# VectorE takes a token block's forget gates one step later in the projection of a hybrid decoder trunk

## The reference, cut to what matters

```
h = rms_norm(x, norm_pre) * (1 + scale) + shift
u = h @ w_in
q, k, v, f_logit, z_rwkv, p_pool, g = jnp.split(u, IN_IDX, axis=-1)
...
log_f = jax.nn.log_sigmoid(f_logit + f_bias)     # 8 forget gates a token, one for each attention head
...
zf = z_rwkv
zf = zf + (token_shift(zf) - zf) * mu            # each token's column is mixed with that of the token before
```

## Time and profile before

| | |
|---|---|
| median of 3 runs | 3588.36 us |
| lowest, highest | 3586.56 us, 3593.07 us |
| the profiled execution's own time | 3581.05 us |
| its span, first to last instruction | 3579.3 us |
| TensorE busy | 3312.7 us, 93% of the span |
| VectorE busy | 2415.0 us, 67% |
| ScalarE busy | 1970.1 us, 55% |
| GpSimd busy | 1785.0 us, 50% |
| mean granted TensorE clock | 0.96 of full speed |

### The profile page before, as it was taken

One profiled execution on the slowest core, in us unless ns is written; L12 is line 12 of the kernel. 1 busy time (PEld: TensorE's weight loads), 2 busy tenths in 40 slices (PEclk: granted clock), 3 DMA queues, 4 the chain that ended last, 5 costly groups with the idle time before them and its releaser, 6 DMA issues. The chain is left out here.

```text
span 3579.3 us, 90138 instructions
## 1 busy us (share of the span) xinstructions
PE 3312.7 (93%) x31944; PEld 2298.4 (64%) x31944; DVE 2415.0 (67%) x4337; ACT 1970.1 (55%) x3745; POOL 1785.0 (50%) x2083
## 2 busy tenths in 40 slices
PE   6788999999999994999998699999999999979998
PEld 6783488469549642888888366666666656644444
DVE  5787756326433335786873789899889988965554
ACT  2444544424432234676775477777777777753333
POOL 2376300510330233344553599889988889852222
PEclk9899999999999997898997899999999999989999
DMA  7387445435444533232210312021120220215555
GB/s 313 129 300 254 161 146 169 151 130 178 146 141 155 181 133 89 57 84 69 67 49 28 70 43 59 9 57 36 29 59 10 55 49 17 58 70 181 186 186 180
DMA packets 247770, 401.06 MB, mean 112 GB/s; under 512 B 85646, under 2 KB 199013, under 8 KB 232453
## 3 DMA queue, kind: packets, MB, share of 16 engines
q1 hardware_dynamic: 223979, 383.75, 33.5%
q10 hardware_dynamic: 22880, 11.54, 1.2%
q0 software_dynamic: 480, 0.14, 0.1%
HBM read 272.77 MB, written 122.59 MB: 110 GB/s over the span
## 5 line engine op out<-in xcount | busy, mean ns | idle before, releaser
L2530 ACT ACTIVATE p<-psc,xb,sc 128x512 f32<-128x512 f32 (+3 forms) x1152 | 848.5, 744 | 315.1 <-PE psc L2621 302.1
L2508 POOL TENSOR_TENSOR plo<-p 128x512 f16<-128x512 f32 (+2 forms) x864 | 906.8, 1078 | 66.9 <-ACT p L2530 65.8
L2677 DVE TENSOR_REDUCE mx<-pm 128x1 f32<-128x512 f32 (+3 forms) x1201 | 731.4, 636 | 99.4 <-PE pm L2552 85.8
L646 PE MATMUL bank<-h,ring 128*128 128x512 f16 x2688 | 597.8, 381 | 4.9 <-DVE u L990 4.9
L2600 PE MATMUL po<-v,p 128*128 128x129 f16 x4224 | 513.3, 220 | 20.9 <-POOL plo L2508 18.0
L651 PE MATMUL bank<-ring,h 128*128 128x128 f16 x8064 | 467.0, 222 | 26.7 <-ACT c L818 12.3
L646 PEld LDWEIGHTS bank<-h,ring 128*128 128x128 f16 x2688 | 263.9, 98 | 343.4 <-issue 42.5
L2602 PE MATMUL po<-v,plo 128*128 128x65 f16 x4224 | 483.4, 192 | 0.0
L651 PEld LDWEIGHTS bank<-ring,h 128*128 128x128 f16 x8064 | 463.6, 99 | 28.1 <-issue 12.6
L2600 PEld LDWEIGHTS po<-v,p 128*128 128x128 bf16 x4224 | 388.8, 97 | 121.3 <-POOL plo L2508 28.0
L2602 PEld LDWEIGHTS po<-v,plo 128*128 128x128 f16 x4224 | 379.2, 98 | 96.2
(11 more groups left out here) (417 smaller groups left out, 5583.3 us busy)
## 6 DMA issues: line engine op xcount, KB each, us to landing
ring<-scratch_ws SPq DMA_DIRECT2D x52, 1792.0 KB, 7.8
scratch_z<-stage SPq DMA_DIRECT2D x72, 256.0 KB, 3.2
scratch_ws<-h SPq DMA_DIRECT2D x10, 1792.0 KB, 6.7
y<-scratch_y SPq DMA_DIRECT2D x35, 512.0 KB
g<-scratch_g SPq DMA_DIRECT2D x35, 512.0 KB
xr<-in_x SPq DMA_DIRECT2D x34, 512.0 KB, 6.2
scratch_g<-stage SPq DMA_DIRECT2D x64, 256.0 KB, 6.0
scratch_qk<-stage SPq DMA_DIRECT2D x64, 256.0 KB, 2.6
```

The costliest lines, as they stand in the source:

```text
L646: t = nc.tensor.matmul(bank[b][:], m.ring[:, slot, l, bo, k, :], hh[:, side, r, ao, k, :], start=fresh and first, stop=last, skip_group_ch ...
L2508: nc.gpsimd.tensor_tensor(plo[:, k % NP, 0:w], p32[:, k % NP, 0:w], hi[:, 0:w], ALU.subtract)\
L2530: nc.scalar.activation(p32[:, k % NP, 0:w], psc[k % 2][:, 0:w], ACT.Exp, bias=xb[:, u, b, x // 4:x // 4 + 1], scale=m.sc[:, 0:1]).then_inc ...
L2677: nc.vector.tensor_reduce(mx[:, s, t, q:q + 1], pm[g][:, 0, 0:w], AX.X, ALU.max).then_inc(pm_d.sem, 1)
```

## The change

The call of `forget` for a token block moves from VectorE's step g, the block's step 0, to step g+1. There it stands behind the shifts of that step, which are those of the last two z tiles of the preceding block. Both lists of VectorE hold the same instructions.

```
@@ -1105,10 +1105,10 @@
                     if group_at(g - 1, 3) is not None:
                         x_scaled(*group_at(g - 1, 3))
-                    if at is not None:
-                        if at[1] == 0:
-                            forget(at[0])
-                        elif at[2] == 1:
+                    if sub(g - 1) is not None and sub(g - 1)[1] == 0:
+                        forget(sub(g - 1)[0])
+                    if at is not None and at[1]:
+                        if at[2] == 1:
                             first_sum(at[0], at[1])
                         elif at[2] == 2:
                             second_sum(at[0], at[1])
```

## The result

| | before | changed |
|---|---|---|
| median | 3588.19 us, 8 runs | 3568.61 us, 8 runs |
| lowest, highest | 3572.18, 3605.60 us | 3557.29, 3576.50 us |
| the profiled execution's own time, its span | 3581.05, 3579.3 us | 3563.71, 3562.0 us |
| mean granted clock in the profiled execution | 0.960 | 0.961 |

The ratio is 0.9946, with a 95% interval from 0.9921 to 0.9972: the change makes the kernel faster, by 19.6 us between the medians. 11.2 us were forecast.

What follows compares the result with a forecast made beforehand. TensorE, busy for 93% of the span, was taken to bound the kernel; 7.0 us of idle time plus 4.2 us of clock, 11.2 us, off the median 3588.36 gave 3577.2 us, range 3570 to 3586.

Steps and rivals of the forecast that it cites:

- Which wait bounds, and what replaces it: Boundaries of blocks 1 to 3: ScalarE's copy would wait for TensorE alone, idle time falling from 3.67 to 1.33 us.
- The term of 2.34 us a boundary: TensorE's idle time behind step 0 in blocks 1 to 3: 2.34 us saved at each, 7.0 us in all.
- The shifts, the gates, the stores: Projection boundaries: shifts run 12 us sooner, forget gates run during ScalarE's copies, stores go out early; gates and stores cost 0.
- The clock, 4.2 us: Behind step 0 of blocks 1 to 3: of 5.9 us lost to half clock, 4.2 us come back.
- one of the three falls: Clock at the boundaries of blocks 1 to 3: one fall to half clock still happens, at 1.7 us.
- the wrong row to fear: Block 0, where the clock fell behind 1.33 us of idle time: nearest row, saying none of the clock loss returns.
- The sum: Projection: 7.0 us of idle time plus 4.2 us of clock, 11.2 us saved in all.
- How the numbers follow, the scatter: Whole kernel: range 3570 to 3586 us, its lower end from 12.9 us of gain and some 4 us of scatter.
- The second term of the range: Whole kernel: a gain of at most 12.9 us, used for the range's lower end.
- The slower rival: Later stages, 1377 to 1900 us: more half-clock stretches, about 1.7 us per fall; 3596 us with eleven; chance 0.08.
- eleven more falls: Later stages: eleven additional clock falls at about 1.7 us each would bring the time to 3596 us.
- The chances: Whole kernel: 0.61 faster (a time under 3581.2 us), 0.31 the same, 0.08 slower.

Runs made afterwards that it cites:

- filled kernel: The kernel before with 11 matmuls added on TensorE behind step 0 in token blocks 1 to 3; medians 3570.85 us (ratio 0.9961) and 3584.58 us (0.9970).
- e3: The changed kernel, with SyncE holding the stores of the preceding block's last two z tiles until TensorE has ended step 0; one run, 3572.44 us.
- e6: The changed kernel ended behind the projection, with x copied to the output instead of the later stages; median 1411.72 us.
- e10: The changed kernel run again as a plain copy with a profile; median 3573.26 us, ratio 0.9932 to the kernel before.
- e12: The changed kernel run once more as a plain copy; median 3576.73 us, ratio 0.9949 to the kernel before.
- e13: The changed kernel run yet again as a plain copy; median 3580.46 us, ratio 0.9956 to the kernel before.
- e5: The kernel before ended behind the projection, with x copied to the output instead of the later stages; median 1424.03 us.
- e9: The kernel before run again as a plain copy with a profile; median 3586.63 us, ratio 0.9994 to the other runs of the same kernel.
- e1: The kernel before with the forget gates moved to the later step in token block 1 alone; one run, 3594.57 us.

## Why the prediction was right and where it was wrong

*Which wait bounds, and what replaces it*: right. All three boundaries now look as block 0 did, with TensorE as the releaser and 1.27 us of idle time (1.33 in block 0). The term of 2.34 us a boundary measured 2.40 by rows, 2.41 by block 3 of the filled kernel.

*The shifts, the gates, the stores*: right. The shifts of the last two tiles begin 10.6, 12.4 and 12.9 us before the end of step 0 (12 forecast), and the gates run beside the copies at no cost. The stores left SyncE at 474.51 in block 1, and ScalarE had to wait for their landing until 485.29, 1.81 us instead of 0.96; TensorE did not notice, and neither did it in e3. From issue to landing the early stores of 256 KB took 10.0 us behind 2.8 MB of loads; in the kernel before, issued at 484.13, they took 2.0. The rule of the Trainium skill that a ring is served in order ("DMA: Bandwidth & Descriptors", section "Queues, rings and completion order") would have it so, and the trace agrees.

*The clock, 4.2 us*: right in kind, off in both halves. I took one of the three falls to stay. None did, in any of five profiles of the changed projection (the first, e6, e10, e12, e13), so the boundaries gave back all that was lost there: 4.79 − 2.40 = 2.4 us in block 1, 4.04 − 2.40 = 1.6 in block 3, and in block 2, by its undisturbed length of 296.24, also 300.26 − 296.24 − 2.40 = 1.6; 5.6 to 5.7 in all, against 5.9 taken. Yet a fall came elsewhere in each of these profiles, behind the 2 us of idle time at about 630 or 925 us, once in four of them and twice in e13, and took 1.4 to 1.9. The kernel before kept its clock at both places in its first profile (the earlier trace rows and the line at 933 us above) and in e5; in e9 it lost it at 634 us. Counted over all profiles, that is 1 of 6 such places in the kernel before and 14 of 24 in the twelve profiles of kernels that have no fall at the boundaries. Whether the one brings the other is not shown. The rule of the Trainium skill that the moment of a switch varies from run to run ("TensorE: Matmul & The Clock Gate", section "What's actually happening") fits these two places. At the boundaries whether the clock fell never varied; for how long it did: in e9 the clock averages 0.69 in the first 5 us after 488 us, where in the first profile it was 0.50 throughout, and in block 2 it stood at 0.50 for 5.5 us after 789.4 us, where in the first profile it averages 0.66 over 5 us. Block 0 was the wrong row to fear; that longer idle times had come before there is the likely reason, but no run tests it.

*The sum*: right for the projection. 11.2 us were forecast; 11.3 came out by the ends of the two projections in the first profiles, 11.6 by the blocks of e5 and e6, 12.3 by their medians. That it fits to a tenth is in part luck: the boundaries gave back 1.4 us more of clock than taken, and the fall elsewhere, which I had not in the sum, took about as much.

*How the numbers follow, the scatter*: this is the step that failed. "12.9 us of gain and some 4 us of scatter reach down to 3571 less one, 3570." The only rows on scatter that I had were three runs, 6.5 us apart, and one profiled execution that already lay 7.3 us lower. Single executions of the whole kernel have a standard deviation of 8 to 13 us (9.7 in the last 29 runs of the kernel before), because the recurrence stage takes anything from 606 to 640 us. By this a median of eight runs carries an error of some 4 us by itself, and the median of three, from which the forecast was taken, one of some 7. As an estimate, a fair range around the same forecast was some 3560 to 3594, twice as wide as the one given. The second term of the range, the gain of at most 12.9 us, may have failed too: it puts the effect on the later stages at nothing, and the mean difference over all runs is 17.9 us with a standard error of 2.2. No profile shows such an effect, so this part stays open.

*The slower rival* put its finger on the right place, the clock behind 1377 us, but undersized it: eleven more falls, 18.7 us, where 31.5 us lie between two executions of one kernel. It was wrong to treat it as one case with a chance of 0.08 beside the others. It is a draw that every single execution makes, in both directions.

*The chances*: faster, at 0.61, is what came. Of the 19.6 us between the medians 11 to 12 are the projection's; the rest is not explained.

## What to carry to other kernels

A wait that looks harmless, since the waiting engine is nowhere near its limit, costs what is queued behind it. Look in each engine's list for work that is ready but stands behind an instruction that waits for the bounding engine, and move it in front. A gap on TensorE costs more than its length when the clock falls behind it; price the gap and the half-clock work separately, and test them apart by filling the gap (here 2.4 us and 1.6 us in block 3). Before giving a range, ask which stage makes the scatter, and where it is far from the change, measure with that stage cut off.

## What the runs showed of the hardware that was not expected

- The lengths of blocks 1 to 3 repeat to 0.01 us in some executions (297.63 or 297.64 us for block 1 in six profiles of four kernels), and what differs between executions comes mostly in steps of 1.4 to 1.9 us, one for each fall of the clock.
- Behind 1.27 us of idle time after step 0 the clock stayed at 1.00 at all 28 boundaries of blocks 1 to 3 in ten profiles (the changed, the filled and the late-store kernels, and block 1 of e1). Behind 3.67 us it fell at all 11 in four profiles (the kernel before, e5, e9, and blocks 2 and 3 of e1). Behind 2.0 us, at about 630 and 925 us, it fell at 16 of 32 places in all sixteen profiles.
- In the recurrence stage the same matmuls were busy for 527.1 us in one execution and 561.1 in another of the same kernel.
